# An encoder step with two thirds of its memory traffic in expert gathers: opening on one token tile in 64-token blocks, and gather units of two heads by one block

## The reference: what is computed

```python
h = rmsnorm(x, ln1_g)
q_a, k_a, v_a, q_i, k_i, w_i, q_b, k_b, v_b, g_b = split(h @ w_in)
o_a = sparse attention: score = sum_h w_i[h] * relu(q_i[h] . k_i), block-causal in chunks of 64,
      the best 64 (tiles 0, 1) or 132 (tile 2) keys of each token, softmax over those, times v_a
o_b = retention (4 heads, decay masks), group-normalised, times silu(g_b)
x = x + concat(o_a, o_b) @ w_out
h2 = rmsnorm(x, ln2_g)
q = h2 @ w_query                      # 8 heads of 256 = 2 halves of 128
v1, i1 = top_k(q[:, :, 0] @ keys1.T, 16);  v2, i2 = top_k(q[:, :, 1] @ keys2.T, 16)
top_s, e = top_k(all 256 sums v1 + v2, 16)          # 16 experts of 16,384 per token and head
f = sum over 8 heads x 16 experts of softmax(top_s) * gelu(u[e] . h2) * v[e]
y = rmsnorm(x + f, ln_final_g)
```

## Time and profile before

| | |
|---|---|
| runs without the profiler | 1157.68 us median of 3 (1155.9 to 1158.31) |
| profiled execution, span from first to last instruction | 1155.1 us |
| bytes moved | 458.68 MB, 397 GB/s over the span |
| of these the gathers' queue | 402.68 MB |
| PE, DVE, ACT, POOL busy | 76%, 71%, 39%, 48% of the span |
| mean granted TensorE clock | 0.884 |

### The profile page before, as it was taken

How to read it: one execution, slowest core, us unless ns; L and a number is a source line. 1 busy time by engine, 2 the same in 40 slices (tenths; PEclk the granted TensorE clock), 3 DMA queues, 4 the chain that set the end, 5 groups by cost and what they waited for, 6 DMA issues and landing times.

```text
span 1155.1 us, 12183 instructions
## 1 busy us (share of the span) xinstructions
PE 875.5 (76%) x3735; PEld 397.5 (34%) x3740; DVE 816.8 (71%) x2123; ACT 448.7 (39%) x1413; POOL 553.4 (48%) x437
## 2 busy tenths in 40 slices
PE   8999988997888857665677768587656667666556
PEld 6748644443333424232233333143222122221111
DVE  2426877876686979996777785757886777767544
ACT  2121444433443424433554663343333333333334
POOL 0002444552554745553564563655474554555443
PEclk9999999999997988897898899888898778877779
DMA  9902999999999999999999999999999999999996
GB/s 378 401 1 78 427 424 426 426 426 429 394 422 428 406 427 426 376 421 423 428 427 424 426 427 427 425 427 425 419 380 426 426 427 426 427 426 427 428 426 274
DMA packets 67079, 458.68 MB, mean 397 GB/s; under 512 B 8387, under 2 KB 10179, under 8 KB 15686
## 3 DMA queue, kind: packets, MB, share of 16 engines
q0 software_dynamic: 55888, 402.68, 83.3%
q1 hardware_dynamic: 10982, 54.97, 11.7%
q10 hardware_dynamic: 144, 0.26, 0.1%
HBM read 453.59 MB, written 3.24 MB: 395 GB/s over the span
## 4 chain that ended last, share of the span: by engine, by line
DMA 41%; PE 26%; DVE 16%; POOL 7%; issue 6%; ACT 3%; SPq 0%; POOLq 0%; DVEq 0%
DMA rows<-in_uv,ids 39%; PE ps L581 25%; DVE rows L1991 8%; POOL rows L520 5%; POOL work L505 1%; ACT work L1212 1%; DMA rows<-in_w_qi 1%; ACT wgt L1212 1%; DMA wt<-in_w_q 1%; DMA rows<-in_uv,last_ids 1%; PE ps L584 1%; DVE top L1581 1%; ACT zact L1212 1%; DVE wt L1585 1%; DVE work L1714 0%
## 5 line engine op out<-in xcount | busy, mean ns | idle before, releaser
L520 POOL DMA_INDIRECT rows<-in_uv,ids x380 | 454.1, 1195 | 471.0 <-PE ps L581 402.7
L581 PE MATMUL ps<-rows,work 128*64 128x512 f32 x1536 | 463.1, 733 | 262.5 <-ACT work L1212 261.8
L1991 DVE CUSTOM_DVE_ANT_0 rows<-rows,wt 128x1024 f32<-128x1024 f32 x256 | 314.0, 1227 | 168.5 <-DMA rows<-in_uv,ids 165.0
L1212 ACT ACTIVATE zact<-zdot 128x1 f32<-128x1 f32 x384 | 77.6, 202 | 555.7 <-DVE zdot L1991 555.2
L581 PEld LDWEIGHTS ps<-rows,work 128*64 128x64 f32 x1536 | 107.1, 155 | 525.2 <-ACT work L1212 366.1
L1991 DVE CUSTOM_DVE_ANT_0 rows<-rows,masks 128x1024 f32<-128x1024 f32 x128 | 157.3, 1231 | 51.4 <-DMA rows<-in_uv,ids 48.5
L581 PE MATMUL ps<-wt 128*128 128x128 f32 (+7 forms) x599 | 155.9, 414 | 0.9 <-DMA wt<-in_w_kv 0.9
L1212 ACT ACTIVATE work<-pair,wgt 128x64 f32<-128x64 f32 x384 | 133.5, 348 | 12.5
L1212 ACT ACTIVATE wgt<-zact,gates 128x1 f32<-128x1 f32 x384 | 113.1, 295 | 12.4
L581 PEld LDWEIGHTS ps<-wt 128*128 128x128 f32 (+2 forms) x604 | 89.2, 192 | 55.1 <-issue 46.9
L581 PEld LDWEIGHTS ps<-work,wt 128*128 128x128 f32 (+1 forms) x664 | 85.1, 203 | 55.7 <-issue 55.7
(11 more groups left out here) (168 smaller groups left out, 679.0 us busy)
## 6 DMA issues: line engine op xcount, KB each, us to landing
wt<-in_w_q SPq DMA_DIRECT2D x8, 2048.0 KB, 12.2
rows<-in_uv,ids POOLq DMA_INDIRECT x380, 12.4
rows<-in_w_out SPq DMA_DIRECT2D x2, 2048.0 KB, 32.2
wt<-in_w_out SPq DMA_DIRECT2D x2, 2048.0 KB, 11.8
wt<-in_ckv SPq DMA_DIRECT2D x16, 256.0 KB, 11.0
x<-in_x SPq DMA_DIRECT2D x5, 512.0 KB, 8.6
rows<-in_w_qi SPq DMA_DIRECT2D x1, 2048.0 KB, 12.9
wt<-in_w_qa SPq DMA_DIRECT2D x1, 2048.0 KB, 11.9
```

The lines of the kernel that those rows point to most:

```text
L520: pool.indirect_dma_start(row[s], None, a["uv"], bass.IndirectOffsetOnAxis(ap=ids[:, own(n // KP).start + n % KP:own(n // KP).start + n % ...
L581: return nc.tensor.matmul(out, lhsT, rhs, start=start, stop=stop)
L1212: return nc.scalar.activation(*args, **kw)
L1991: V.tensor_tensor_reduce(row[s][:, 0:D], row[s][:, 0:D], h2r[t][:, n % 2, :], 1.0, 0.0, ALU.mult, ALU.add, zdot[:, s:s + 1]).then_inc(dott ...
```

## The change

1. **The opening takes tile 0 alone.** Keys, values, index queries, attention queries of tiles 1 and 2 go behind the first gathers (`opening_rest`, `later_keys`, `index_1`), on ticks 0 to 50. The whole list of later work moves back by some 22 to 24 ticks (`PROJECTIONS` begins at 38, not 14; tile 2's index rounds at 121, not 92).
2. **64-token blocks in the opening.** Tokens 0 to 63 attend without an index; the index is made for tokens 64 to 127 only; w_out, second norm, queries and top 16 are made for block 0, then block 1. Two matmuls of 64 output columns stand side by side for the two halves.
3. **Units of two heads by one block.** Partition = (head, token of the block), so ids and gates are found where they are used and `spread_out`, `spread_take` go. There are 24 units as before. Scores are made for two units at a time (`scores_at(g)`).
4. **Packed sums.** A block's output is one PSUM bank, columns 0 to 511 in partitions 0 to 63, the others in 64 to 127. `acc` counts single gathers. The sum of squares of the last norm needs a matmul with `pair`.
5. **Buffers.** Gathers 0 to 7 have four, 8 to 19 six, from 20 on eight. Gather 0 waits for w_out of both blocks, 8 for the queries of heads 2 and 3, 20 for all index queries. Behind gather 3 POOL waits for keys and values of tile 2.
6. **Loads.** ln1_g no longer as a 512 KB broadcast but as 16 rows, transposed to `gT`; w_qa and w_qkb ahead of the small tables; `load_q(1)` is issued in the opening.

Cut to its core:

```diff
+        def slot_of(n):
+            return n % 4 if n < 8 else (n - 4) % 6 if n < 20 else (n - 14) % 8
+        HURRIED, FAST = (4, 5, 6, 7, 8, 9, 10, 11, 16, 17), (2, 4, 8, 16)
+        def q_at(hd):
+            return {2: 2, 3: 4, 4: 32, 5: 38, 6: 48, 7: 56, 8: 96, 9: 102, 10: 116, 11: 124, 16: 228, 17: 232,
+                    18: 238, 19: 246}.get(hd, 16 * hd - 56 + hd % 2 * -4)
+        def top16_at(u):
+            return {2: 10, 3: 30, 4: 47, 6: 67, 8: 111, 10: 133, 16: 240, 18: 263}.get(u, 16 * u - 27 + u % 2 * -2)
...
 # SP
             load_q(0)
+            sp.wait_ge(kv_sb, 1)
+            outputs_kv(0)
+            sp.wait_ge(sqd, 3)
+            sp.dma_start(g2b, a["ln2_g"].partition_broadcast(P)).then_inc(g2b_in, 16)
+            repeat_h2(0)
+            load_q(1)                                   # waits qn_ps 2
+            sp.wait_ge(wout, 2)
+            sp.dma_start(x[:, 0, :], a["dmask"]).then_inc(tables_in, 16)
+            repeat_h2(1)
...
 # POOL, gather(n)
-                if n == 4:
-                    pool.wait_ge(qi_ps, 3)
-                if n == 6:
+                if n == 0:
+                    pool.wait_ge(wout, 2)
+                if n == 8:
                     pool.wait_ge(q_ps, 2)
-                if n >= G:
-                    pool.wait_ge(acc, (n - G) // 2 + 1)
+                if n == 20:
+                    pool.wait_ge(qi_ps, 4)
+                if before(n) >= 0:
+                    pool.wait_ge(acc, before(n) + 1)
 # POOL, loop
+                if n == 3:
+                    pool.wait_ge(kv_ps, TILES)
+                    pool.memset(wz, 0.0).then_inc(wz_zero, 1)
...
 # PE, end of the opening
+            def out_0(b, c0, c1):
+                for c in range(c0, c1):
+                    for e in range(2):
+                        last = mm(ps[64 * e:64 * e + 64, 6 + b, :], mixT0[:, c, 64 * b:64 * b + 64], w_out0[e][:, c, :], False, c == KC - 1)
+            block_t(0); y_begin(0); out_0(1, 2, 4); block_sum(0)
+            block_queries(0); out_0(1, 4, 6); block_queries_t(0); out_0(1, 6, 8)
+            unit_scores(0)
+            block_t(1); y_begin(1); block_sum(1)
+            norm_t(1, xn12[0], (0, 3))
+            block_queries(1); block_queries_t(1)
+            norm_t(2, xn12[1], (1, 2))
+            unit_scores(1)
+            natural(1, w_kv, 0, NKV).then_inc(kv_ps, 1)
 # PE, ticks: opening_rest
+                natural(2, w_kv, 1, NKV).then_inc(kv_ps, 1)      # tick 0
+                yield from until(6)                              # 6, 8, 10, 12: index queries, tiles 1 and 2 at once
+                joint_index_queries(0)
...
+                dots_1(0)                                        # 14 to 26: dots, sums, attention queries
...
 # PE, add_experts
-                for e in range(2):
-                    for j in range(2):
-                        last = mm(ps[64 * j:64 * j + 64, Y_BANK[..] + e, :], diag[:, s, :], row[s][:, D + e * 512:D + (e + 1) * 512], False, stop)
-                last.then_inc(acc, 1)
+                for j in range(2):
+                    for e in range(2):
+                        last = add_expert(n + j, e, ..)
+                    last.then_inc(acc, 1)
 # the last two gathers: for e: wait for its part of v; add_expert(n, e); add_expert(n + 1, e)
...
 # DVE, top16_ids
+                V.scalar_tensor_tensor(ids[:, own(u)], half_id[:, 0, :], float(NK), half_id[:, 1, :], ALU.mult, ALU.add)
-                for j in range(2):
-                    ins = V.tensor_scalar(spread[:, j, :, :], flat, side[:, j:j + 1], None, ALU.mult)
-                then(ins, chosen)
-            def spread_take(u): ...
 # DVE, index_2: one half round on every tick from 121
                 for r in range(0, TOPK[2], 8):
-                    yield
-                    if r % 32 == 24:
-                        yield
                     for part in range(2):
                         yield
                         score_round(score2, r, TOPK[2], part)
```

More of the change, by code:

```diff
@@ new lines, in block_queries, with block_queries_t @@
+            def block_queries(b):
+                for c in range(KC):
+                    for h in range(2):
+                        last = mm(ps[64 * h:64 * h + 64, 4, 0:256], h2T[:, c, 64 * b:64 * b + 64],
+                                  w_q(0)[:, c, 256 * h:256 * h + 256], c == 0, c == KC - 1)
+                last.then_inc(qn_ps, 1)
+            def block_queries_t(b):
+                pe.wait_ge(qn_sb, b + 1)
+                for e in range(2):
+                    last = tr(ps[:, 4, 256 + e * P:256 + (e + 1) * P], qn[:, e * P:(e + 1) * P])
+                last.then_inc(q0_ps, 1)
@@ new lines, in unit_scores, with y_begin @@
+            def unit_scores(u):
+                b = u % 2
+                for e in range(2):
+                    last = mm(sc_psum(b, e), qT[:, e, b, :, :], keysT[:, e, :])
+                last.then_inc(sc2_ps, 1)
+            def y_begin(b):
+                mm(ps[:, 6 + b, :], ident[:], xp[b], True, False)
+            pe.wait_ge(xp_set, 1)
+            block_t(0)
+            y_begin(0)
+            out_0(1, 2, 4)
+            pe.wait_ge(small_in, 16 * 7)
+            block_sum(0)
+            pe.wait_ge(h2t_dve, 1)
@@ L960, in retention_1, with out_1 @@
+            def out_1(e, c0, c1):
+                for c in range(c0, c1):
+                    last = mm(ps[:, 1 + e, :], mixT[:, c, :], w_out[e][:, c, :], c == 0, c == KC - 1)
+                if c1 == KC:
+                    last.then_inc(wout, 1)
             def retention_1():
-                yield from until(26)
+                yield from until(52)
                 pe.wait_ge(rotated, 2)
+                pe.wait_ge(pv_sb, ATT[2])
                 for s in range(4):
@@ L1035, in retention_2 @@
                     if h == 1:
-                        yield from until(114)
+                        yield from until(134)
             def states_2():
@@ new lines, in index_2 @@
+                pe.wait_ge(mt_sb, 2)
+                mm(ps[:, 0, 0:P], e8[64:64 + HI, :], wT2).then_inc(w_ps, 1)
+                yield from until(84)
+                dots_2(0)
+                dots_2(1)
+                yield from until(88)
+                sums_2(0)
+                dots_2(2)
+                yield from until(92)
+                h2_t(1)
+                yield from until(96)
+                sums_2(1)
+                sums_2(2)
+                dots_2(3)
+                dots_2(4)
@@ new lines, in _ @@
+            exps_0(0)
+            act.wait_ge(qi_ps, 2)
+            for e in range(2):
+                ins = copy(qiT0[0:64, :, 4 * e:4 * e + 4, :].rearrange("p g j t -> p j g t"),
+                           ps[64 * e:64 * e + 64, 4, 256:512].rearrange("p (j g t) -> p j g t", j=4, g=4))
+            ins.then_inc(qi_sb, 1)
+            act.wait_ge(dots, 1)
+            A(relu0, ps[:, 0, :], ACT.Relu).then_inc(relued, 1)
+            act.wait_ge(pt_ps, 1)
+            copy(probT0[0][0:64, :], ps[0:64, 1, :]).then_inc(pt_sb, 1)
@@ new lines, in index_1 @@
+            def index_1():
+                yield from until(24)
+                dve.wait_ge(summed, CACHE)
+                then(V.tensor_copy(score1[:, 0:P], ps[:, 1, 256:256 + P]))
+                then(V.tensor_tensor(score1[:, P:2 * P], ps[:, 1, 256 + P:512], bar[:, 0:P], ALU.add), scored)
+                for r in range(0, TOPK[1], 8):
+                    score_round(score1, r, TOPK[1], 0)
+                    score_round(score1, r, TOPK[1], 1)
+                    if r % 16:
+                        yield
+                set_bias(bias1, score1)
@@ L1906, in retention_2 @@
                 set_qz(1)
-                yield from until(110)
+                yield from until(129)
                 dve.wait_ge(s_ps, 3)
@@ L1984, in _ @@
+            def finals():
+                yield from until(139)
+                last_mean(0, 0, 2)
+                yield from until(267)
+                last_mean(1, 2, 4)
+                for m in range(4):
+                    yield from until(276 + 4 * m)
+                    last_normed(m, m // 2)
+                yield from until(377)
+                last_mean(2, 4, 5)
+            gens = (next_top16(), later_keys(), index_1(), background(), index_2(), finals())
             for n in range(UNITS * KP):
-                t, s = n // (HP * KP), n % G
```

1501 lines of the change are left out of this document (798 added, 703 removed).

## The result

| | before | after |
|---|---|---|
| median of the runs, us | 1157.99 (1155.9 to 1158.88) | 1200.49 (1198.9 to 1202.23) |
| span of the profiled execution, us | 1155.1 | 1197.6 |
| MB moved | 458.68 | 458.43 |
| transfer at 427 GB/s, us | 1074.2 | 1073.6 |
| rest of the span, in which nothing was moved, us | 80.9 | 124.0 |

The changed kernel is slower: 1.0374 times the time before, 95% interval 1.036 to 1.0388. Forecast were 1153 and a range from 1143 to 1162. The bytes came out as forecast; 43 us of pauses came on top of those of the kernel before.

What follows compares the result with a forecast made beforehand. DMA transfer was taken as the bound: 1074.2 us at 427 GB/s plus 80.9 us of pauses. 1155.1 - 5.8 + 0.9 + 0.7 - 0.6 = 1150.3 us span; the median lies 2.6 above: 1153 us, range 1143 to 1162.

Steps and rivals of the forecast that it cites:

- The opening: Up to the first gather: following PE's work, gather 0 issues at 94.3 us where it was 110.13, 15.8 us earlier.
- more is gained: Rival, 1144 us, chance 0.22: 256-column pairs cost near 1.7 for 3.9, and rows 0 and 1 land 5.6 us after issue.
- What the first gathers do: Gathers 0 to 7: four buffers make the DMA idle; 47.3 us lost where it was 53.1, 5.8 gained.
- Gathers 8 to 30: PE's 62 us of work run 6 us behind the data, covered by the buffers: 0 to 3 us, 0.9 taken.
- The later list unchanged: Later work moves by 22 to 24 ticks with the same pieces and loads; the other pauses keep their price.
- The rounds of tile 2: Tile 2's index rounds on all 34 ticks: DVE 106.8 us against DMA 98.4; 3.9 us lost, the same as before.
- a cushion of buffers: In tile 2's index rounds: about four of eight buffers in the DMA's queue, absorbing 8 to 10 us.
- The slower rival: Rival, 1162 us, chance 0.18: DVE's list at 121 to 155 is the bound; nothing of 8.4 us is absorbed.
- The tail and the bytes: Kernel's end: last gathers add in the same 64 columns, + 0.7 us; 0.52 MB less, 0.26 MB more, - 0.6 us.
- signs of being wrong: First gather later than 100 us, DMA dips between rows 8 and 60, or pauses behind row 60 not 21 +- 3.
- No change: Rival, 1156 to 1158 us, chance 0.15: the four-buffer phase eats all, by dearer 64-wide entries or gathers 4 to 7 landing later.
- a dearer entry into 64-wide work: Half of "No change": each of the opening's 16 entries costs 0.2 to 0.3 us above 0.22, 3 to 5 us.

Runs made afterwards that it cites:

- e2: The changed kernel with keys and values of tile 2 taken ahead of the gather loop, ACT's copy following at once: 1194.04 us.
- e5: The changed kernel with keys and values of tile 2 and the queries of heads 2 and 3 taken ahead of the gather loop: 1187.43 us.
- e3: The changed kernel with ACT's and DVE's readers of PE's pieces up to tick 26 moved to the third row behind; a few PE steps move too: 1190.46 us.
- e6: e5 with joint index queries also started on PE's first tick and ACT's and DVE's readers on the third row behind each piece: 1161.62 us.
- e10: e6 with the readers on ACT and DVE as near behind PE's pieces as in the changed kernel: 1181.31 us.
- e13: e9 with DVE's rotation of tile 1 one row later (41 for 40): 1159.62 us.
- e15: e6 with tile 2's index scores pulled together, queries of heads 4 and 5 at rows 28 and 34, DVE's rotation of tile 1 one row later: 1156.11 us.
- e9: e6 with every step between tile 1's index selection and tile 2's index scores 4 rows earlier: 1163.6 us.
- e8: The changed kernel with 5 or 6 of the 8 matmuls left out of each of the six later projections: 1195.07 us.
- e7: The changed kernel with 8 of the 17 rounds of tile 2's index selection left out, the rest spread over the same rows: 1192.83 us.
- e4: The changed kernel with matmuls of zeros ahead of each of the first 17 pairs on PE, from a new 64-byte tile: 1209.86 us.

## Why the prediction was wrong, step by step

**The opening: right.** Gather 0 was forecast at 94.3 and went at 92.51 us. Eight pairs of 256 columns, for which the trace of before had no row, took 3.67 us; the sum had 3.9, and "more is gained" 1.7.

**"What the first gathers do": right places, too small.** 47.3 us were forecast from the last load (55.3 us) to 133. 53.7 are lost from 57 to 140, as many as before (53.4 by the same rows), and the 1.3 lost more ahead of 57 belong to it too: the whole gain of the opening is spent. Gather 4 was named with its wait (114.2, measured 119.20), gather 8 with its own (131, measured 138.07). Of the first 5 us, 2.8 are the start of row 1's addition (109.18 and not 106.4). Row 1's product began at 106.95 where the row was to land at 104: the DMA moved 350 GB/s from 95 to 110 us at a busy share of 0.98, where the forecast had 427. The rest is PE. The addition takes 3.68 and not 1.94, keys and values 5.13 and not 4.65, behind 12.8 us of idle, with a granted clock of 0.50 from 100 to 110 us. The prices on PE had been read where PE was full. e2 and e5 confirm the two waits: the first taken out gives 6.4 us, both together 13.1.

**"Gathers 8 to 30": this is the step that failed.** 0.9 us were forecast, with PE over 95% busy from 130 to 190; 20.7 are lost from 140 to 200 us and 5.8 from there to 260, with PE busy 45.17 of 60 us. PE's pieces up to tick 26 were to end at 191.7 us and ended at 228.1. The step summed PE's work (62 us) and set it against the transfer, as if PE were limited by its sum alone. It never placed the readers: that ACT copies index queries on row 10 and 13, and DVE the keys on row 12, stood in the code and wasn't set against the pieces on PE's ticks 8, 10 and 12. The runs showed in its place that PE waits 3 to 4 us for those readers ahead of each pair and then works at half clock. e3, in which little but the readers moves, takes 10.0 us off, and e6 against e10 19.7. In the kernel before most of these pieces and their readers run ahead of the gathers, where a reader that waits holds up no row. What e3 leaves from 140 to 200 us (8.9 lost) isn't assigned, and from 200 to 260 PE also waits 3.2 us for w_q of head 4, which the forecast didn't have.

**"The later list unchanged": wrong by some 8 us.** 10.5 are lost from 260 to 340 us (2.2 before). e13 and e15 show a reader two rows behind its piece to be worth 3 to 4 us in kernels with that same list, and the changed kernel has its wait (11.19 us on DVE) in this stretch; the rest I can't assign: e9 moved it elsewhere, and e8 shows only that less PE work removes 5.

**The rounds of tile 2: mis-sized.** 3.9 were forecast "again", 10.8 are lost. The surplus of 8.4 us of DVE work had been worked out, and then given to a cushion of buffers; 6.9 of it weren't absorbed. The slower rival (nothing absorbed, 12.3 lost) came nearer here. e7 gives 7.7 for half of the rounds. DVE was 96 to 97% busy from 500 to 520 and from 550 to 580 us, where much of the loss stands, but 87% from 460 to 600. (The four terms of the sum come to 105.9 and not 106.8, so the surplus was 7.5. In the same way the two gains of "more is gained", 4.4 and 4, are 8.4 and not 8.8. Neither changes the argument.)

**The tail and the bytes: right.** The last 17 us and the fraction behind them lose 10.8 (10.1 before), the 0.7 forecast, and 458.43 MB are 0.6 us less of transfer.

Of the rivals, "slower: 1162" named one true mechanism, worth 7 of the 43 us. Two of the signs of being wrong that the prediction named came true: DMA dips between rows 8 and 60, and a sum of the later pauses that isn't 21 +- 3 (28.0 us from 340 us on; row 60 is added at 328.8). "No change" had the four-buffer phase eating all, which it did; a dearer entry into 64-wide work, its other half, isn't seen: gather 0 came 1.8 us earlier than with 0.22 us for each. The Trainium skill, TensorEngine Tiling (Array Packing), Key Properties, says that a change of tiling mode drains the engine. With a full instruction lost on each change gather 0 would have come near 104, an estimate (94.3 and the 10 of the prediction); it came at 92.51, so the trace doesn't bear out a drain of that size.

## What to carry to other kernels

When work moves in among a stream of gathers, place its readers as well as the work: for each piece, name the row on which each other engine's list waits for it, and what stands behind that wait. Here a reader that stood before the last row that the next addition needed turned two engines that overlap into one chain, and one to three rows more took most of PE's wait away. Work for an idle stretch may be taken from just behind it: 12 us of PE's, put under DVE's top 16, were worth 13.1 us here (e5).

## What the runs showed of the hardware

- Behind 12.8 us of PE idle, the 8 instructions of a pair took 3.68 us and not 1.94; the granted clock was 0.50 from 100 to 110 us. In the turns with 3 to 4 us of idle they took 2.8 to 3.7; with none, in e3, 1.94 again. Behind idle of 1.3 to 1.5 us both are seen in the changed kernel (1.94 at 139.06, 3.44 at 189.17 us). So a wait on PE cost its length and up to 1.7 us on the next pair.
- In e4 the DMA moved 418 to 421 GB/s where it moved 425 to 427 in the changed kernel, at the same share of busy time and with the same bytes (458.46 and 458.43 MB). By these rates it cost some 9 us over 620 (340 to 460, 600 to 820 and 900 to 1180 us). Known of it is only that all tiles behind one of 64 bytes lay elsewhere; it is one trace, though all four runs of e4 were slower than those of the changed kernel.
